# Two kinds of stores move from the sync engine's DMA queue to ScalarE's

## What is computed

```python
def one_block(xb):                                   # 128 tokens
    q = (xb @ w_pq).reshape(TOK_BLOCK, PEER_HEADS, 2, D_KEY_HALF)
    s = jnp.einsum('thcd,hcnd->thcn', q, sub_keys).astype(jnp.float32)
    s1, i1 = lax.top_k(s[:, :, 0], PEER_TOPK)
    s2, i2 = lax.top_k(s[:, :, 1], PEER_TOPK)
    ...                                              # 16 best of the 256 sums
    g = jax.nn.softmax(top_s, axis=-1)
    u = jnp.take(u_exp, eidx, axis=0)                # 16384 experts of width 1024
    a = jax.nn.gelu(jnp.einsum('thkd,td->thk', u, xb).astype(jnp.float32))
    w = (g * a).astype(xb.dtype)
    return jnp.einsum('thk,thkd->td', w, jnp.take(v_exp, eidx, axis=0))
```

## Time and profile before

| | |
|---|---|
| median of 3 runs | 4145.35 us (4144.81 to 4147.48) |
| the profiled execution | 4145.56 us, span 4143.8 us |
| TensorE busy, mean granted clock | 94%, 0.983 of full speed |
| VectorE, GpSimd, ScalarE busy | 68%, 54%, 41% |
| DMA queue of SP / of POOL / of ACT | 630.7 / 335.6 / 3.2 MB |
| gelu stores, SP | 256 of 240 KB, 2.9 us from issue to landing (median) |
| gate stores, SP | 60 of 1024 KB, 4.7 us |

### The profile page before, as it was taken

One profiled execution on the slowest core, in us unless ns is written; L12 is line 12 of the kernel. 1 busy time (PEld: TensorE's weight loads), 2 busy tenths in 40 slices (PEclk: granted clock), 3 DMA queues, 4 the chain that ended last, 5 costly groups with the idle time before them and its releaser, 6 DMA issues.

```text
span 4143.8 us, 57586 instructions
## 1 busy us (share of the span) xinstructions
PE 3886.4 (94%) x21170; PEld 3362.8 (81%) x21170; DVE 2826.8 (68%) x4491; ACT 1696.9 (41%) x2936; POOL 2232.5 (54%) x1240
## 2 busy tenths in 40 slices
PE   7978899999999999999979989999999999999997
PEld 5756898888888888878769989888888888788876
DVE  3774227988875588888863322788887548888886
ACT  3264324556666322222231132455666632222223
POOL 1101234665556677777742323465565667777774
PEclk9999999999999999999999999999999999999998
DMA  5302224778888998898945312477888889988994
GB/s 201 124 1 110 100 99 164 249 269 284 292 299 309 314 307 303 301 314 297 316 147 182 107 57 92 160 243 258 280 300 282 311 312 306 314 295 299 313 316 160
DMA packets 395800, 972.44 MB, mean 235 GB/s; under 512 B 32048, under 2 KB 221232, under 8 KB 381744
## 3 DMA queue, kind: packets, MB, share of 16 engines
q1 hardware_dynamic: 301664, 630.72, 45.2%
q0 software_dynamic: 92160, 335.59, 22.7%
q10 hardware_dynamic: 1744, 3.21, 0.2%
HBM read 835.37 MB, written 133.96 MB: 234 GB/s over the span
## 4 chain that ended last, share of the span: by engine, by line
issue 41%; POOL 34%; PE 17%; DMA 4%; DVE 3%; ACT 1%; POOLq 0%; DVEq 0%; ACTq 0%
POOL SL L444 18%; POOL ROWS L451 14%; PE PS L762 10%; PE PS L564 5%; POOL SL L435 3%; DMA ROWS<-u_exp,EI 2%; DMA ROWS<-v_exp,EI 1%; PE PS L754 1%; DVE ROWS L1267 1%; PE PS L715 1%; DVE OH L1256 0%; DVE PO L1193 0%; ACT SH L995 0%; PE PS L774 0%; DVE TS L1188 0%
## 5 line engine op out<-in xcount | busy, mean ns | idle before, releaser
L444 POOL TENSOR_TENSOR SL<-RW,SH 128x1024 fp32r<-128x1024 f32 x512 | 1284.0, 2508 | 928.6 <-ACT SH L995 887.7
L774 PE MATMUL PS<-WH,SH 128*128 128x480 f32 x2048 | 786.9, 384 | 63.3 <-DVE WL L1317 60.7
L762 PE MATMUL PS<-HH,SH 128*128 128x480 f32 x2048 | 804.5, 393 | 7.8 <-POOL SL L444 6.5
L995 ACT CAST SH<-RW 128x1024 fp32r<-128x1024 f32 x512 | 535.9, 1047 | 613.8 <-PE PS L762 514.1
L762 PE MATMUL PS<-HL,SH 128*128 128x480 f32 x2048 | 780.0, 381 | 0.0
L762 PE MATMUL PS<-HH,SL 128*128 128x480 f32 x2048 | 779.8, 381 | 0.0
L774 PE MATMUL PS<-WH,SL 128*128 128x480 f32 x2048 | 777.2, 379 | 0.0
L774 PE MATMUL PS<-WL,SH 128*128 128x480 f32 x2048 | 776.9, 379 | 0.0
L435 POOL TENSOR_TENSOR SL<-RW,SH 128x1024 fp32r<-128x1024 f32 x84 | 202.5, 2414 | 815.8 <-ACT SH L819 815.8
L1034 ACT CAST WH<-GL 128x480 fp32r<-128x480 f32 x256 | 152.0, 594 | 938.1 <-DVE GL L1311 934.0
L1273 DVE SCALAR_TENSOR_TENSOR ACC<-ROWS,AA,ACC 128x1024 f32<-128x1024 f32 x256 | 399.1, 1559 | 186.8 <-DMA ROWS<-v_exp,EI 174.4
(11 more groups left out here) (171 smaller groups left out, 5358.6 us busy)
## 6 DMA issues: line engine op xcount, KB each, us to landing
RW<-u_blk SPq DMA_DIRECT2D x256, 512.0 KB, 4.3
RW<-v_blk SPq DMA_DIRECT2D x256, 512.0 KB, 5.5
gate_acts<-GE SPq DMA_DIRECT2D x256, 240.0 KB, 2.9
router_weights<-GT SPq DMA_DIRECT2D x60, 1024.0 KB, 4.7
GB<-router_weights SPq DMA_DIRECT2D x32, 1920.0 KB, 12.7
GL<-gate_acts SPq DMA_DIRECT2D x256, 240.0 KB, 4.7
RW<-wstream SPq DMA_DIRECT2D x100, 512.0 KB, 4.5
AW<-wpairs SPq DMA_DIRECT2D x40, 1024.0 KB, 5.2
```

The costliest lines, as they stand in the source:

```text
L444: nc.gpsimd.tensor_tensor(SL[:, r % 2], RW[:, r % RAW], SH[:, r % 2].bitcast(F32), ALU.subtract).then_inc(raw_used, 1)
L762: last = mm(PS[:, n % 2, NG:NS], w[:, n % 2, j], a[:, j, NG:NS], start=(j == 0 and q == 0), stop=(j == DJ - 1 and q == 2))
L774: last = mm(PS[:, dj, NG:NS], w[:, k % 2, dj], a[:, k, NG:NS], start=start, stop=stop)
L995: nc.scalar.copy(SH[:, r % 2], RW[:, r % RAW]).then_inc(hi_done, 1)
```

## The change

The two helpers `store_gelu` and `store_gates` leave SP's program and stand in ACT's, with the same waits and the same buffers. ACT stores the gelu of block n - 2 in iteration n between `high(n + 1)` and `gelu(n - 1)`, and a group of gates right behind the `layout` of its last quad. The last two gelu blocks are stored behind the last gelu and behind the first `high` of the v sweep.

```diff
@@ sync engine, experts(l)
-            def store_gelu(n):
-                sp.wait_ge(gelu_done, 2 + l * NB_E + n + 1)
-                sp.dma_start(ge_dram[n], GE[:, n % 4, NG:NS]).then_inc(ge_out[n % 4], 16)
-
-            def store_gates(tg):
-                sp.wait_ge(gt_done, 2 + l * NQ + (tg + 1) * (TG // 4))
-                sp.dma_start(g_dram[tg], GT[:, tg % 2]).then_inc(gw_done[tg % 2], 16)
...
             for n in range(NB_E):
                 expert_chunk(n + 3)
-                if n >= 2:
-                    store_gelu(n - 2)
-                for tg in range(NTG):
-                    if QUAD_BLOCK[tg * (TG // 4) + TG // 4 - 1] == n - 2:
-                        store_gates(tg)
                 if n == QUAD_BLOCK[-1] + 3:
                     load_gates(0)
                     for b in range(4):
                         load_gelu(b)
             for n in range(NB_E):
-                if n < 2:
-                    store_gelu(NB_E - 2 + n)
                 expert_chunk(NB_E + n + 3)
@@ ScalarE, experts(l)
+            def store_gelu(n):
+                act.wait_ge(gelu_done, 2 + l * NB_E + n + 1)
+                act.dma_start(ge_dram[n], GE[:, n % 4, NG:NS]).then_inc(ge_out[n % 4], 16)
+
+            def store_gates(tg):
+                act.wait_ge(gt_done, 2 + l * NQ + (tg + 1) * (TG // 4))
+                act.dma_start(g_dram[tg], GT[:, tg % 2]).then_inc(gw_done[tg % 2], 16)
...
+                if n > 1:
+                    store_gelu(n - 2)
                 if n > 0:
                     gelu(n - 1)
                     for g in QUADS_AT[n - 1]:
                         layout(g)
+                        if g % 4 == 3:
+                            store_gates(g // 4)
                 for g in QUADS_AT[n]:
                     gates(g)
...
             gelu(NB_E - 1)
+            store_gelu(NB_E - 2)
             for n in range(NB_E):
                 if n < NB_E - 1:
                     high(NB_E + n + 1)
+                if n == 0:
+                    store_gelu(NB_E - 1)
                 w_high(n + 2)
```

## The result

| | median of 5 runs | span of the profiled execution |
|---|---|---|
| before | 4146.58 us (4144.81 to 4149.64) | 4143.8 us |
| changed kernel | 4167.98 us (4164.76 to 4174.50) | 4166.2 us |

The ratio is 1.0054 (95% interval 1.0041 to 1.0067), 21 us slower. I had forecast 4146.4, a range of 4138 to 4158, and "slower" with 0.13. Two runs of experiment 2 (4523.26 and 16645.49 us) and one of the kernel before beside experiments 1 to 4 (12166.92 us) were slow runs, far from all others, and stand in no median or ratio here.

What follows compares the result with a forecast made beforehand. TensorE (busy 3886.4 of 4143.8 us) was taken to set the pace. 4145.6 + 0 + 0 + 1 + 0 = 4146.6 for the profiled execution, stated as 4146.4 us; own range 4141 to 4151, wider range 4138 to 4158.

Steps and rivals of the forecast that it cites:

- SP loses its stores: Sync queue: 256 and 60 stores of 0.32 us leave, 101 us of an idle sequencer, worth 0.
- Gelu stores on ACT: ScalarE, 256 stores: 0.4 us issue each, hidden under the 1.05 us cast, so gelu starts on time; cost 0.
- gate stores: ScalarE, 60 stores: `gates` starts 0.7 us late, with at least 1.68 us before PE's first use; cost 0.
- The second rival: ScalarE: store issue takes 1 us or more and is not covered; +12 us, 4157; chance 0.06.
- The third: Turn between sweeps: ACT's store gets stuck where SP is stuck; at most +4.6 us for two layers, 4150; chance 0.10.
- The DMA engines: First sweeps: bytes unchanged, stores, chunks and gathers share differently; +1 us taken, bounds -10 and +20.
- the ten PE waits: First sweeps: ten of 26 PE waits preceded by a gather wait, some 10 us; each 2 us later gives +20.
- a sum above 160 us per layer: Sign for the fourth rival: DVE's wait for u gathers above 160 us per layer, forecast near 128.
- fourth rival: Gathers: with three queues they get a smaller part while gate store and chunk run; 4166; chance 0.07.
- The first rival: Loads and gathers no longer stand behind stores; up to -10 and -5.5 us, with most of it 4133; chance 0.09.
- The bytes ahead of a gather are the same in either arrangement; only the sharing differs.: Gathers near a gate store: same bytes ahead of them before and after the move; part of the +1 us term.
- The turn: Between the sweeps: gate load up to 0.8 us earlier, against stores sharing the engines; 0 taken, bounds -5.5 and +4.6.

Runs made afterwards that it cites:

- experiment 2: Changed kernel with the gelu stores back on the sync engine, so only the 60 gate stores are on ScalarE: 4147.09 us, ratio 0.9995 to the kernel before.
- experiments 1 to 4: Four kernels with part of the move: only gelu stores (4167.74 us), only gate stores (4147.09), all but the turn's gelu stores (4162.26), only the turn's gelu stores (4153.70).
- 5: Gelu stores on ScalarE's queue but at the old moment, 1.5 us after the cast starts; gate stores on the sync engine: 4147.86 us, ratio 1.0004 to the kernel before.
- 3: Changed kernel with the gelu stores of blocks 118 to 127 back on the sync engine in the old order: 4162.26 us, ratio 1.0037 to the kernel before.
- 8: All stores on the sync engine's queue, gelu stores issued at the changed kernel's early moment: 4162.05 us, ratio 1.0039 to the kernel before.
- 9: Kernel before with each gelu store issued later, directly ahead of the next chunk, 3.6 us after the cast starts: 4155.96 us, ratio 1.0015.
- Experiment 4: Kernel before with only the gelu stores of blocks 118 to 127 on ScalarE's queue, ten per layer: 4153.70 us, ratio 1.0016.
- 6: Kernel before with the turn's first gate load and four gelu loads three blocks later: 4141.43 us, ratio 0.9987.

## Why the prediction was wrong

**SP loses its stores: worth 0.** Right: 2 and 5 are at 0.

**Gelu stores on ACT, cost 0; gate stores, 0.7 us each under cover, cost 0.** Right in mechanism and size: 0.33 us per issue, `gates` 0.63 us late, experiment 2 at 0.9995, and 5, with the gelu issues on ACT, at 1.0004. The slack of 1.68 us and more was enough. The second rival (issue not covered) is out. The third (ACT stuck where SP is stuck) is out as well: while SP's four gelu loads of the turn take 11.25 us, ACT issues two stores in 0.33 us each.

```profile
1380.70 11.25 SPq L356 DMA_DIRECT2D GL<-gate_acts  x4
...
1384.16 0.33 ACTq L1023 DMA_DIRECT2D gate_acts<-GE  x1
...
1389.38 0.33 ACTq L1023 DMA_DIRECT2D gate_acts<-GE  x1
```

**The DMA engines: "+1, for the gelu stores now meet the first gather of a block and not only the second".** This is the step that failed, in size: 1 us was forecast and 15 us measured (3 and 8). The direction and the place (the moment within the block) were in the sentence, but I priced it from the ten PE waits that had a gather wait shortly ahead of them. That count is the wrong multiplier. (15 lies inside the +20 that I named as a bound, but I gave the rival that stood for it 0.07.) In the sweeps VectorE's waits for gathers grew from 248.7 us in 121 waits to 264.9 us in 150, and TensorE's idle time from 42.4 to 50.0 us; over five kernels of either moment it is 8.9 us more, and the lower clock takes 3.4 us more, a term that the forecast didn't have. My own sign for this rival, a sum above 160 us per layer, would never have shown. That TensorE's idle time comes from the late gathers by way of VectorE's one-hots is argued: its waits for them grow with it (37.7 and 44.4 us), but in 9 the gathers are as late and TensorE loses little. The experiments at one moment on either queue (5 against 8) show the moment alone. My fourth rival put the harm in the third queue and the gate stores; it had nearly the right size of time (4166), for a reason that experiments 2 and 5 exclude. The first rival (relief for gathers and loads) is out.

**"The bytes ahead of a gather are the same in either arrangement; only the sharing differs."** True of the gate stores (2: nothing). Not true of the gelu stores, which came 1.5 us forward in the block.

**The turn: "I take 0; bounds -5.5 and +4.6".** Failed too: 6.6 us. I saw that SP's last store ahead of the gate load goes away and that "the stores of two blocks now share the engines with the load", and set one against the other. Counted from the cast of block 118, the load was issued 0.5 and 1.1 us earlier in the two layers, about as said, but the cast of the late chunk began 3.0 and 4.3 us later. Before, those stores stood in line behind the gate load and the chunks that TensorE needed; on their own queue they overtook them. Experiment 4 prices it at 6.6 us, 2 above my bound. What I also left out is the granted clock: a wait of PE of 4.8 us came with 6.9 us at the lower of its two levels, 1.2 GHz.

Sum: 0 + 0 + 15 (3 or 8) + 6.6 (4) = 21.6, measured 21; by 5, with its 1.7, the turn would be smaller and the sum 17, at the lower end of the measured interval (17 to 28).

The Trainium skill, "DMA: Bandwidth & Descriptors", section "Issuing engines are not separate DMA queues", says that the issuing engine only changes who spends the issue time. In the sweep the runs agree (5: 1.0004 on ACT's queue). At the turn 4 doesn't: ten stores per layer on a queue of their own cost 6.6 us, where order in the queue had been a priority.

Open: why the median of 5 shows so little of its long turns; why a store issued at the top of the block slows the gathers although it lands no earlier than one issued 1.5 us later; and how much of TensorE's idle time is due to those gathers. The traces show the facts and not what the DMA engines do in between.

## What to carry to other kernels

When a DMA is moved to another engine, ask first at what moment it will be issued, and only then from which queue; keep the moment and the move is free in the sweep (5), keep the queue and move the moment and most of the cost is there (8: 15 of 21 us). One queue for urgent loads and patient stores is an order of priority: a store that may overtake a load needs a reason, and a load that may wait (6) should not stand ahead of one that may not. If the engine whose waits are counted is fed through a second engine, the few waits that lead straight from one to the other are not a bound on what a delay costs: here they gave 1 us where 15 were measured. And idle time of TensorE can bring a lower granted clock with it, which is a term of its own. To compare stretches of two kernels, cut them at the same work, not at the same time.

## What the hardware showed that I had not expected

- ScalarE issues a plain 128-row store in 0.33 us, as the sync engine does (0.32), and while it computes. The 0.62 us of the earlier trace rows belong to the small transfer EI<-EI.
- While SP is stuck for 11 us, a DMA on ACT is issued in 0.33 us.
- Issuing a 240 KB store 1.5 us earlier, into engines busy with gathers, made it take 5.1 us instead of 3.4 and the second gathers 0.5 to 0.6 us longer.
- 240 KB more per block at the better of the two moments still cost 16 us for 212 stores, though the DMA engines' mean busy share from 600 to 1362 us was 0.76 before and 0.82 with them (263 and 289 GB/s).
- The 7560 matmuls between the same blocks of the two sweeps keep TensorE busy for 1449 to 1454 us in all fourteen kernels, once the loss to the lower clock level is taken off; the sweeps differ by idle time and clock.
